# Other PSUM banks, another order and a second load queue in an RWKV scan; norm and rotations moved beside the products of the second block's mixers

## The reference, cut to what matters

```python
# first block: one of two mixers is RWKV-7, 8 heads of 64, run in both directions
def step(S, inp):
    r_t, w_t, k_t, v_t, kk_t, b_t = inp
    sa = jnp.einsum('bhij,bhj->bhi', S, -kk_t)
    S = (S * w_t[:, :, None, :] + sa[..., None] * b_t[:, :, None, :]
         + v_t[..., None] * k_t[:, :, None, :])
    return S, jnp.einsum('bhij,bhj->bhi', S, r_t)
y = (rwkv7_scan(r_h, heads(decay[:, :, 0]), k_h, v_h, kk, b_h, False)
     + rwkv7_scan(r_h, heads(decay[:, :, 1]), k_h, v_h, kk, b_h, True))
...
# second block: attention over a window and 256 context tokens, beside a convolution
qx, kx, vx, ux = split_proj(hx @ w_in[i])
kvc = hc @ w_in[i][:, ATT_DIM:3 * ATT_DIM]
qx_rot = axial_rope(qx, row_pos, col_pos)
kx_rot = axial_rope(kx, row_pos, col_pos)
attn_x = neighbourhood_attention(qx_rot, qx, kx_rot, vx, kc, vc, rpb[i])
conv_x = conformer_conv(ux, dw_kernel[i], dw_bias[i], conv_ln_g[i], conv_ln_b[i])
#   conv_x: h = a * sigmoid(b), 31 taps per channel + bias, layer norm over channels, silu
x_new = x + g1 * (jnp.concatenate([attn_x, conv_x], axis=-1) @ w_out[i])
```

## Time and profile before

| | |
|---|---|
| median of 3 runs | 3825.01 us (3813.8, 3825.01, 3825.13) |
| profiled execution | 3817.68 us, its span 3816.4 us |
| PE busy | 3333.0 us, 87% |
| DVE busy | 2303.4 us, 60% |
| ACT busy | 988.7 us, 26% |
| POOL busy | 416.9 us, 11% |
| TensorE clock granted, mean | 0.92 of full speed |

### The profile page before, as it was taken

One profiled execution on the slowest core, in us unless ns is written; L12 is line 12 of the kernel. 1 busy time (PEld: TensorE's weight loads), 2 busy tenths in 40 slices (PEclk: granted clock), 3 DMA queues, 4 the chain that ended last, 5 costly groups with the idle time before them and its releaser, 6 DMA issues.

```text
span 3816.4 us, 56694 instructions
## 1 busy us (share of the span) xinstructions
PE 3333.0 (87%) x24667; PEld 2751.8 (72%) x24667; DVE 2303.4 (60%) x3149; ACT 988.7 (26%) x1464; POOL 416.9 (11%) x218
## 2 busy tenths in 40 slices
PE   7988797578887699999999887995888979999997
PEld 5777685367776377888888676783667768888885
DVE  5768475367775444444444565995555656666666
ACT  4543142121110222111111343112445311121122
POOL 2510053000000400000000122220000101111110
PEclk9998798589998699999999998997999989999998
DMA  4400254112111211111111212104000111111111
GB/s 135 131 28 10 67 165 129 35 31 36 29 36 44 94 66 28 50 50 50 50 50 50 77 39 72 45 28 96 1 1 3 54 57 49 45 56 45 46 54 61
DMA packets 261824, 209.29 MB, mean 55 GB/s; under 512 B 87001, under 2 KB 223976, under 8 KB 260936
## 3 DMA queue, kind: packets, MB, share of 16 engines
q1 hardware_dynamic: 247751, 180.50, 16.1%
q10 hardware_dynamic: 13824, 25.17, 2.1%
HBM read 172.84 MB, written 30.95 MB: 53 GB/s over the span
## 4 chain that ended last, share of the span: by engine, by line
PE 70%; DVE 17%; ACT 6%; DMA 2%; POOL 2%; SPq 2%; issue 2%; DVEq 0%; ACTq 0%; POOLq 0%
PE ps L1922 22%; PE ps L1937 15%; PE ps L1785 5%; PE ps L614 4%; PE ps L615 4%; PE ps L616 4%; PE ps L2599 2%; PE ps L1359 2%; PE ps L2577 2%; DVE s_Z L1528 2%; DVE s_tmp L1527 2%; DVE Yc L2506 2%; PE ps L669 1%; PE ps L2587 1%; SPq L1333 1%
## 5 line engine op out<-in xcount | busy, mean ns | idle before, releaser
L2895 DVE TENSOR_TENSOR H<-H,ps 128x1024 f32<-128x1024 f32 x256 | 312.6, 1221 | 182.5 <-PE ps L1937 175.7
L2087 DVE TENSOR_TENSOR fsum<-fsum,ps 128x1024 f32<-128x1024 f32 x168 | 205.1, 1221 | 311.6 <-PE ps L1937 309.4
L1937 PE MATMUL ps<-dh,hh 128*128 128x512 f32 x864 | 340.3, 394 | 17.9 <-DVE hl L1902 13.2
L1937 PE MATMUL ps<-dl,hh 128*128 128x512 f32 x864 | 338.9, 392 | 0.0
L1937 PE MATMUL ps<-dh,hl 128*128 128x512 f32 x864 | 338.9, 392 | 0.0
L1922 PE MATMUL ps<-hn_h,uh 128*128 128x512 f32 x704 | 275.6, 392 | 7.0 <-DVE ul L1626 4.6
L1922 PE MATMUL ps<-hn_l,uh 128*128 128x512 f32 x704 | 274.9, 391 | 0.0
L1922 PE MATMUL ps<-hn_h,ul 128*128 128x512 f32 x704 | 274.8, 390 | 0.0
L1922 PE MATMUL ps<-hx_h,uh 128*128 128x512 f32 x512 | 201.2, 393 | 7.8 <-DVE hx_l L1902 5.3
L1937 PEld LDWEIGHTS ps<-dh,hh 128*128 128x128 f32 x864 | 163.9, 190 | 55.9 <-DVE hl L1902 14.4
L1922 PE MATMUL ps<-hx_l,uh 128*128 128x512 f32 x512 | 201.1, 393 | 0.0
(11 more groups left out here) (473 smaller groups left out, 7734.2 us busy)
## 6 DMA issues: line engine op xcount, KB each, us to landing
aw<-in_w_ada_dram ACTq DMA_DIRECT2D x96, 256.0 KB, 2.9
uw<-in_w_mlp_dram SPq DMA_DIRECT2D x32, 512.0 KB, 4.2
dw<-in_w_mlp_dram SPq DMA_DIRECT2D x32, 512.0 KB, 5.2
uw<-in_ffn_gate_dram SPq DMA_DIRECT2D x22, 512.0 KB, 4.0
uw<-in_ffn_up_dram SPq DMA_DIRECT2D x22, 512.0 KB, 5.3
dw<-in_ffn_down_dram SPq DMA_DIRECT2D x22, 512.0 KB, 6.0
cw<-in_w_in_dram SPq DMA_DIRECT2D x20, 512.0 KB, 3.9
o_w<-in_w_out_dram SPq DMA_DIRECT2D x16, 512.0 KB, 13.5
```

The lines of the kernel that those rows point to most:

```text
L1937: mm = pe.e.matmul(ps[:, 2 * pair + hf, :], v[s][:, blk(t)], w[:, half(hf)], start=(m == 0), stop=(m == 2))
L2087: return dve.c.tensor_tensor(f, f, new, ALU.add) if g else dve.c.tensor_copy(f, new)
L2895: return dve.c.tensor_tensor(h, h, self.ps[:, 4 + 2 * (t % 2):6 + 2 * (t % 2), :], ALU.add)
```

## The change

In the scan: `yy` is in bank 2 of its direction and no longer waits for `S`. `cum` comes right behind `yy`, then `p4` (bank 1), and only then `tr` and the two levels (`l4` in bank 0, `p5` and `l5` in bank 1). Of the 8 loads of `ZZ`, SP issues the four even ones and ACT the four odd ones, on a counter of their own (`t_zb`). `products` and DVE's order are as before, and `products` still waits for `tr`.

In the mixers: the order of the blocks is gates, v, k, q. DVE makes the low parts of the weights instead of POOL. DVE's taps are dealt out by a list, so many behind each block. The sums of the norm and the rotations are done behind blocks 13 to 19. Gain and bias of the norm are in ACT's silu. The rotation writes its product in PSUM. POOL clears the three tiles of attention; the mask is added to each quarter of the bias table just before its first use.

```diff
@@ mixers2, POOL: now three memsets behind block 19
-        self.mixers2_pool()
+        self.pool.wait_ge(self.pe["u", 19])
+        for x in (self.Qb, self.Qc, self.ob):
+            self.pool.e.memset(x[:], 0.0).then_inc(*self.pool.one("ob0"))
@@ rwkv_scan_sp
-            for k in range(8):
-                sp.e.dma_start(self.ZZ[n % 2][...], zd[n % 2, k]...).then_inc(*self.t_z.one("in", n))
+            self.inverse_back(sp, self.t_z, n, range(0, 8, 2))
@@ rwkv_scan_pe
             if u >= 0:
                 for d in range(2):
-                    pe.wait_ge(dve["S", u, d])
-                    self.heads_pe(d, 3, CH, 0, (...), "yy", u, d)
+                    self.heads_pe(d, 2, CH, 0, (...), "yy", u, d)
+            if u % 2 == 0 and (u + 4) // 2 < NBLK:
+                if u >= 0:
+                    pe.wait_ge(act["U", u, 1], dve["y", u, 1])
+                else:
+                    pe.wait_ge(act["Ei", 0, 1])
+                self.cum_pe((u + 4) // 2)
+            if 0 <= m < NSUB:
+                pe.wait_ge(self.t_z["in", m], self.t_zb["in", m])
+                for d in range(2):
+                    ...
+                    self.heads_pe(d, 1, CH, 0, (...), "p4", m, d)
             if n < NSUB:
                 for d in range(2):
                     pe.wait_ge(dve["nm", n, d])
                     ...
                     tr.then_inc(*pe.one("tr", n, d))
             if 0 <= m < NSUB:
-                (p4 stood here, in bank 0; cum behind l4; l4 in bank 1, p5 in bank 0)
@@ rwkv_scan_act, behind U
+            if 0 <= u + 1 < NSUB:
+                act.wait_ge(self.t_z["out", u + 1])
+                if u >= 1:
+                    act.wait_ge(pe["l4", u - 1, 1], dve["zz", u - 1, 1])
+                self.inverse_back(act, self.t_zb, u + 1, range(1, 8, 2))
@@ in2_blocks
-        return glu + [w[:, PART * n:PART * (n + 1)] for n in range(12)]
+        return glu + [w[:, PART * n:PART * (n + 1)] for n in (8, 9, 10, 11, 4, 5, 6, 7, 0, 1, 2, 3)]
@@ mixers2_pe: what follows the second half of a block
+        after[13, 1] = lambda: self.swap_pe(4, self.kr[:, 0, :], 6, act["u", 12], act["VV", 3])
+        after[15, 1] = lambda: self.swap_pe(5, self.kr[:, 1, :], 6, act["u", 13], dve["rope", 4])
+        both(16, (self.norm_mean_pe,), (self.swap_pe, 6, self.kr[:, 2, :], 6, act["u", 14], dve["rope", 5]))
+        both(17, (self.norm_sums_pe,), (self.swap_pe, 7, self.kr[:, 3, :], 6, act["u", 15], dve["rope", 6]))
+        both(18, (self.norm_over_pe,), (self.swap_pe, 1, self.q[:, 1, :], 6, act["u", 17], dve["rope", 7]))
+        both(19, (self.swap_pe, 0, self.q[:, 0, :], 4, act["u", 16], dve["conv", 3]),
+             (self.swap_pe, 3, self.q[:, 3, :], 6, act["u", 19], dve["rope", 1]),
+             (self.swap_pe, 2, self.q[:, 2, :], 4, act["u", 18], dve["rope", 0]))
@@ mixers2_dve
+        for s in range(20):
+            dve.wait_ge(pe["u", s])
+            if s + 2 < 20:
+                self.split_low_dve("u", self.cw, self.in2_blocks(), s + 2)
+            if s < 8 and s % 2:
+                ... (the gate's product)
+            if s == 1:
+                context()
+            for _ in range((0, 2, 7, 7, 7, 7, 7, 7, 9, 12, 12, 12, 12, 10, 8, 5, 0, 0, 0, 0)[s]):
+                next(taps)
+            ... (s = 14: rope 4; 15: norm_sum, rope 5; 16: norm_centre, rope 6;
+                 17: norm_inverse, rope 7; 18: norm_scale, rope 1)
+        for c, base in ((0, 4), (3, 6), (2, 4)):
+            rope(c, base)
@@ attention_dve: softmax(t, u)
+            if t == 0 and u < 4:
+                dve.e.tensor_tensor(self.bias[:, u], self.bias[:, u], rep(self.cmask[:], RPB_R), ALU.add)...
```

More of the change, by code:

```diff
@@ L2383, in values_turn_pe, with swap_pe, norm_mean_pe, norm_sums_pe @@
         tr.then_inc(*pe.one("VV", n))
+    def swap_pe(self, c, src, base, *ready):
+        pe = self.pe
+        pe.wait_ge(self.t_misc["swap"], *ready)
+        for h in range(2):
+            mm = pe.e.matmul(self.ps[:, base + h, :], self.swap[:], src[:, half(h)], start=True, stop=True)
+        mm.then_inc(*pe.one("rope", c))
+    def norm_mean_pe(self):
+        pe = self.pe
+        pe.wait_ge(self.dve["ln_sum"], self.act["kvc", 15], self.act["VV", 3])
+        for h in range(2):
+            mm = pe.e.matmul(self.ps[:, 4 + h, :], self.ones[:], self.qr[:, 0, half(h)], start=True, stop=True)
+        mm.then_inc(*pe.one("ln_mean"))
+    def norm_sums_pe(self):
+        pe = self.pe
+        pe.wait_ge(self.dve["ln_sq", 3])
+        for t in range(NBLK):
+            mm = pe.e.matmul(self.ps[:, 4, 2 * t:2 * t + 2], self.qr[:, 1, blk(t)], self.ones[:, 0:2], start=True, stop=True)
+        mm.then_inc(*pe.one("ln", "sums"))
+    def norm_over_pe(self):
+        pe = self.pe
+        pe.wait_ge(self.dve["ln", "wide"])
+        for t in range(NBLK):
+            tr = pe.e.transpose(self.ps[:, 4 + t // 4, (t % 4) * PART:(t % 4 + 1) * PART], self.qr[:, 2, blk(t)], self.ident[:])
+        tr.then_inc(*pe.one("ln", "over"))
     def mixers2_pe(self):
@@ L2390, in evac @@
             return dve["u", j] if j < 8 and j % 2 else act["u", j]
-        after = {(j, 0): (lambda j=j: self.context_product_pe(j)) for j in range(12, 20)}
+        after = {(j, 0): (lambda j=j: self.context_product_pe(j)) for j in range(8, 16)}
         after[0, 0] = lambda: self.hx_turn_pe(NBLK - 2)
@@ L2404, in mixers2_pe @@
[L2404 to L2416, removed]
+        for n in range(4):
+            after[9 + n, 1] = lambda n=n: self.values_turn_pe(n)
@@ L2519, in mixers2_dve @@
-        dve.c.tensor_tensor(mean, mean, self.Yc[:, 2, :], ALU.add).then_inc(*dve.one())
-        dve.c.tensor_tensor(mean, mean, self.Yc[:, 3, :], ALU.add).then_inc(*dve.one("ln_sum"))
-        dve.wait_ge(pe["ln_mean"])
-        for c in range(4):
-            y, sq = self.Yc[:, c, :], inv if c == 0 else tmp[:, c % 2, :]
-            dve.c.scalar_tensor_tensor(out=two(y), in0=ps[:, 6:8, :], scalar=-1.0 / RW, in1=two(y), op0=ALU.mult, op1=ALU.add) \
-                .then_inc(*dve.one("ln_y", c))
-            if c:
-                dve.wait_ge(act["ln_sq", c])
-                dve.c.tensor_tensor(inv, inv, sq, ALU.add).then_inc(*dve.one("ln_sq", c))
@@ L2529, in mixers2_dve @@
-        self.rsqrt_dve("ln", 2 * NBLK, [pe["ln", "sums"]], ALU.mult, 1.0 / RW, ALU.add, 1e-6)
-        self.over_dve("ln", self.st[:, 1, 0:2 * NBLK].rearrange("p (b two) -> p b two", two=2)[:, :, 0:1], tmp[:, 0, :])
-        dve.wait_ge(pe["ln", "over"])
-        for c in range(4):
-            y = self.Yc[:, c, :]
-            dve.c.tensor_tensor(two(y), two(y), ps[:, 6:8, :], ALU.mult).then_inc(*dve.one())
-            dve.c.tensor_scalar(y, y, self.col("conv_ln_g_2", c), self.col("conv_ln_b_2", c), ALU.mult, ALU.add).then_inc(*dve.one("conv", c))
@@ new lines, in mixers2_dve, with norm_sum, norm_centre @@
+        mean, inv, tmp = self.qr[:, 0, :], self.qr[:, 1, :], self.qr[:, 2:4, :]
+        def norm_sum():
+            dve.c.tensor_tensor(mean, self.Yc[:, 0, :], self.Yc[:, 1, :], ALU.add).then_inc(*dve.one())
+            dve.c.tensor_tensor(mean, mean, self.Yc[:, 2, :], ALU.add).then_inc(*dve.one())
+            dve.c.tensor_tensor(mean, mean, self.Yc[:, 3, :], ALU.add).then_inc(*dve.one("ln_sum"))
+        def norm_centre():
+            dve.wait_ge(pe["ln_mean"])
+            for c in range(4):
+                y = self.Yc[:, c, :]
+                dve.e.scalar_tensor_tensor(out=two(y), in0=ps[:, 4:6, :], scalar=-1.0 / RW, in1=two(y), op0=ALU.mult, op1=ALU.add) \
+                    .then_inc(*dve.one("ln_y", c))
+                if c >= 2:
+                    dve.wait_ge(act["ln_sq", c - 1])
+                    dve.c.tensor_tensor(inv, inv, tmp[:, (c - 1) % 2, :], ALU.add).then_inc(*dve.one("ln_sq", c - 1))
+            dve.wait_ge(act["ln_sq", 3])
+            dve.c.tensor_tensor(inv, inv, tmp[:, 1, :], ALU.add).then_inc(*dve.one("ln_sq", 3))
@@ new lines, in norm_inverse, with norm_scale @@
+        def norm_inverse():
+            self.rsqrt_dve("ln", 2 * NBLK, [pe["ln", "sums"]], ALU.mult, 1.0 / RW, ALU.add, 1e-6, src=ps[:, 4, 0:2 * NBLK])
+            self.over_dve("ln", self.st[:, 1, 0:2 * NBLK].rearrange("p (b two) -> p b two", two=2)[:, :, 0:1], tmp[:, 0, :])
+        def norm_scale():
+            dve.wait_ge(pe["ln", "over"])
+            for c in range(4):
+                y = self.Yc[:, c, :]
+                dve.e.tensor_tensor(two(y), two(y), ps[:, 4:6, :], ALU.mult).then_inc(*dve.one("conv", c))
```

212 lines of the change are left out of this document (111 added, 101 removed).

## The result

The changed kernel takes 3849.29 us (median of 5 runs, 3844.32 to 3854.12), the kernel before in the same comparison 3813.8 us: a ratio of 1.0084, 95% interval 1.0060 to 1.0107. By that ratio it is 32 us slower (the two medians lie 35.5 us apart), where I forecast 26 us less. The profiled execution took 3849.29 us (span 3847.9) against 3817.68.

A forecast was written before the change was run, and what follows sets the result against it. Bound in the scan by two nearly equal chains, SP's loads (16.6 us) and DVE's (14.7), in the mixers by the order on DVE and PE; mixers -43 plus scan +17 gives -26, 3825 to 3799 us, range 3776 to 3828.

The forecast's parts named there:

- It must wait for `y` of direction 1 (+3.8 without waits), takes 3.72 us, and ends at +7.5: Scan, turns with `cum`: moved ahead, `cum` ends later than the landing; turn 29.3 us against 28.65, +4 us over six.
- the levels at 5.75 us: Scan: the time from `t4` to the end of `xt`, taken as before the change, 5.75 us a turn.
- C: Rival, scan: PE's clock falls to 1.2 GHz, chain work of about 7 us a turn doubles; 3838 and more; chance 0.05.
- `p4` ahead of `tr`: Scan: DVE's products start at +8.3, not +4.6, behind the landing; 1.7 us more a turn, nine turns, +15.5 us.
- The second queue: Scan: SP issues 4 loads of `ZZ` instead of 8, so they land 2.4 us earlier, +5.8 instead of +8.2.
- Rival A: Scan: the queues hinder each other, the landing stays at +8.2, turns of 30.0 us, scan +45, 3827 us; chance 0.17.
- D: Rival, scan: the products' place costs nothing, landing by +4.5 or so; scan +5, 3787 us and below; chance 0.05.
- rope 4's wait: Mixers: PE stands 10 us behind block 15, waiting for DVE's `rope 4`.
- block 19: Mixers: the last block ends at 2617, 22 us later than before.
- the tail: Mixers, behind block 19: swap 0 (1.9) and three rotations of 3.8; last rotation some 13 us behind the block.
- B: Rival, mixers: taps stay at 1.55 us, 20 us more on PE's wait for `rope 4`, 3818 us; chance 0.13.
- the 2 us for the mask's quarters: Attention's start: four mask quarters, 1.07 each, return in the first softmaxes, the first under a wait; others cost 2 us.

The follow-up runs named there:

- sig_early: The changed kernel with SP issuing the load of `sig` one turn earlier, under the solve: 3814.28 us, ratio 0.9988 to the kernel before.
- tr_first: The changed kernel with `tr` ahead of `cum` and `p4` again, the late load of `sig` kept: 3761.85 us, ratio 0.9852 to the kernel before.
- filler2: The changed kernel with idle matmuls behind `yy` and, in odd turns, 13 more behind `tr`: 3831.03 us, ratio 1.0037 to the kernel before.
- tr_sig: The changed kernel with `tr` ahead of `cum` and `p4` and `sig` loaded a turn earlier: 3719.79 us, ratio 0.9742 to the kernel before.

## Why the prediction was wrong

**The step that failed** is "It must wait for `y` of direction 1 (+3.8 without waits), takes 3.72 us, and ends at +7.5". `cum` has a third input, the load of `sig` (512 KB, SP, behind the loads of `ZZ`). In the kernel before it stands at +6.8 of a turn whose solve ended at 933.51, 4.0 us to its landing in the median:

```profile
940.35 0.45 SPq L1327 DMA_DIRECT2D sig<-sg_dram  x1
```

so it landed near +10.9, and `cum`, behind `l4`, began at +12.7: less than 2 us to spare. Moved to +3.8, `cum` meets a load issued at +3.8 that lands at +7.9. I counted what the moved step issues and waits for on its own engine, and didn't ask where on SP's queue its data is loaded. That is 6.9 us a turn, 41 in all (some 25 for the wait, the rest mostly the low clock of `cum`); sig_early takes back just this, 40.3 us of profiled scan.

**The second step that failed: the levels at 5.75 us, and the clock as a rival with the wrong price.** C had the mechanism ("PE now stands some 4 us between `yy` and `p4`, and again under the products") and 0.05. It doubled all of a turn's PE work on the chain (about 7 us) in the turns that are hit, and took those to be few. All fourteen turns that transpose were hit, each in a part of its PE work: by about 3.8 us in the turn above (21.5 - 17.7). The eight turns without `cum` that still transpose take 30.5 us on the mean against 27.65 predicted: 8 x 2.8 = 23 us. My "against" was a scan at 0.91 with gaps of 2.8 us. The change put `p4` and `tr` together, and PE now stands 4.5 us ahead of them and 3.7 us behind. The turn of the kernel before from which I took the 5.75 us had its full clock:

```profile
961.60:987.50 25.90, 19.15 (x544) 18.33 (x544) 19.89 (x62) 2.73 (x6) 0.00 (x0) 1.00 0.16 26
```

against 0.76 from the end of a solve to the end of `xt` now. But it was not the rule there either. The next turn without `cum` has 0.93, with a gap ahead of `p4` no longer than the 2.78 us of the first:

```profile
1018.30:1044.10 25.80, 20.51 (x544) 19.75 (x544) 19.88 (x64) 2.73 (x6) 0.00 (x0) 0.93 0.16 25
...
1026.38 1.32 PE L1359 MATMUL ps<-s_ZZ,s_NM 64*64 64x64 f32 x32 [2.62 <-DMA s_ZZ<-zd_dram]
```

Of the nine turns without `cum` before, four took 5.7 us from `t4` to the end of `xt`, the other five 7.0 to 7.3; in the changed kernel all fourteen turns that transpose take 7.6 to 7.8. So the kernel before already ran part of its levels at the low clock, and 5.75 us was the best case, not the price of a turn. The Trainium skill has this shape (TensorE: Matmul & The Clock Gate, HAM oscillation — how this bites in real kernels): a loop that waits for a transfer in each step can lose the clock in each step anew. The trace agrees, 0.76 in the stretch that is shown, and the eight turns within 1.3 us of each other.

**What held.** *`p4` ahead of `tr`* costs by the mechanism I gave: DVE stands for the transposes, the products lie behind the landing. tr_first shows it: with the transposes ahead, turns without `cum` fall by 5.5 us, below those of before. How much of a turn's loss is the order alone was not measured; the pieces of filler2 give +17.7 for my +18.3. *The second queue:* landing at +5.9, predicted +5.8; `N16` not waited for. The last turn is 1.8 us shorter (I had 2.4). Rival A is refuted by the simultaneous issues, and D by DVE's 5.9 us on `tr`. The Trainium skill's rule of one shared generator (Perfetto Trace Analysis, DMA Instruction — HWDGE) would have put the landing at +8.2; this case doesn't show such a cost: 4 and 4 issues take 1.78 and 1.86 us side by side.

**The mixers.** -48.9 for -43, each step where it was put: rope 4's wait 8.9 for 10, block 19 ends 18.4 us later for 22, the tail 12.5 for 13, the taps at their short length (B refuted). Block 19 came 3.6 us sooner than I had it, 1 us of which I had counted by itself, and the tail was 1 us shorter; the 2 us for the mask's quarters lie behind the queries, where this count ends.

**The sum.** Predicted +17 and -43. Found in the scan: 41 for the load of `sig`, 37 for the eight turns without `cum` that transpose, 8 for what is left of the six turns with `cum` (forecast 4), and -2 for the last turn: +84. Of the 37, 8 x 1.7 = 14 are the forecast's price of the products' place and 23 the rest, which I put to the low clock; that split is a remainder, not a measurement (by the pieces of filler2 it would be 10 and 26). My own sum had a slip: it took the 1.7 us nine times, but the ninth turn without `cum` is the last, which has no `tr` and for which I counted -2.4 as well, so my terms give +15, not +17. In the mixers -49.

## What to carry to other kernels

When a step is moved ahead, follow each of its inputs back to the queue that loads it, and compare its issue there with the new place; the old place tells nothing of how late a load may come. When a reordering opens gaps on PE, look at the turn as a whole, and at all turns of the trace, not at one: two gaps of some 4 us in one turn took the clock of the work between and behind them. Useful work put there can pay for itself: in tr_sig a turn with `cum`, whose PE has 3.72 us more to do and no gap of a microsecond, is 0.75 us shorter than one without. What a second load queue pays depends on the order around it: 4 us of scan in one, 18 in another.

## What the runs showed of the hardware

- Products that compute nothing made the kernel 21 us faster (3849.29 to 3827.89), with a granted clock of 0.92 instead of 0.83 in the scan.
- The length of PE's gap alone doesn't tell whether the clock falls: in the kernel before the gap of 2.78 us in the turn from 962.16 left 1.00 for the whole turn, and the turn with the gap of 2.62 us, from 1018.33, has 0.93.
- In the kernel before, the eight issues of a turn's `ZZ` take 3.7 to 5.0 us, because in nine of the 16 groups one of them takes 1.2 to 1.7 us where the median is 0.45. In the changed kernel, where DVE and PE stand meanwhile, none is longer than 0.47; in tr_sig, where they work, single ones take up to 2.06 us again, on both queues in the same turn (2.77 and 2.78 us for four). What holds them up was not tried.
